# Nine normalizations of a three-block transformer pass taken in two token halves, with the GEMM blocks around each computed by halves

## The chip, the cores and the metric

The kernel runs on one core of a Trainium2 chip. Its engines are TensorE (PE in the profile, with PEld for its weight loads), VectorE (DVE), ScalarE (ACT), GpSimd (POOL) and SyncE (SP), which issues most DMAs. The metric is the device time of one execution in microseconds, as the median of several runs. Lower is better.

## The reference, cut to what matters

Two latent blocks and one further block are applied to 256 latent tokens, and in the first block to 256 context tokens as well, so 512 tokens ("both") up to the first half of the second block and 256 after it. The width is 1024. All in float32.

```python
x = x + 0.5 * mod[2] * swiglu(modulate(x, gain0, mod[0], mod[1]), ffn_a_in, ffn_a_out)
x = x + mod[5] * mixer(modulate(x, gain1, mod[3], mod[4]))      # attention + hyena, then retention
x = x + 0.5 * mod[8] * swiglu(modulate(x, gain2, mod[6], mod[7]), ffn_b_in, ffn_b_out)
# third block: plain rms_norm in place of modulate, a mixer, a cross attention, two swiglus
def modulate(x, gain, shift, scale):
    return rms_norm(x, gain) * (1 + scale) + shift
def rms_norm(x, gain):                       # over the 1024 features of each token
    return x * rsqrt(mean(x * x, -1) + 1e-6) * gain
```

Every residual update `x = x + gate * (h @ w_out)` is followed by a norm over the features of the whole new x, and that norm's result is the input of the next GEMM.

## The kernel before, in words

**Tiling.** x lies in SBUF with features on the partitions: `X[:, c, token]`, with eight chunks c of 128 features. A GEMM (one entry of `GEMMS`) is cut into blocks of 256 output features; a block has two tiles t of 128 features. Float32 accuracy is had from fp16: each weight tile `W` is split into `WH` (ACT, line 989, times 64) and the remainder `WL` (DVE, line 1362), each input into `XH` and `XL`, and `three` (lines 619 to 626) issues WH·XH, WH·XL, WL·XH. A block over kc chunks is 2·kc·3 matmuls, each with T columns (512 or 256 tokens). Most GEMMs have kc = 8 and so 48 matmuls a block; the outputs of the swiglus have kc = 11 in two parts, so 66 a block and 8 blocks.

**Residual GEMMs** (kind "resid", ten of them) have four output units u of two chunks. The last two units end in the last two blocks. DVE adds each unit to X (`add`, line 1477), ACT squares the new chunks (`squares`, line 1065), and POOL adds the squares of chunks 1 to 6 to that of chunk 0 (`pool_sums`, line 1778).

**The norm.** After the last block, PE adds the squares over the partitions (`pe_sums`, lines 594 and 601: 1 and 8 calls), DVE takes the reciprocal (line 1501), ACT the root (line 1095), PE spreads the result over the partitions (`pe_spread`, line 610: 4 calls). Each call is float32 and shows as two matmul records. Then, for each chunk, DVE multiplies (line 1518, "h"), ACT writes `XH` (line 1105, or 989 where there is no shift), DVE writes `XL` (line 1524 or 1526, "low"). PE's first block of the next GEMM waits for `XL` chunk by chunk; the later blocks don't.

**Order around the norm.** Each engine runs a written order; waits are on counting semaphores. Weights have two slots: the block k of the next GEMM can be split by ACT only when PE has left the same slot, so block 0 of the next GEMM after the second last block (`begin(after, (0,))`), and block 1 after the last (`begin(after, (1,))`). SP loads the next weights as soon as a slot of `W` has been split. In three of the GEMMs PE also computes modulation columns (`pe_mod`, lines 584 and 585) after each block, whose weights ACT and DVE split last after a norm (`begin_mods`).

The nine residual GEMMs named in the change and what follows each: ffn_0a_out (even_u), even_out (ffn_0b_in), ffn_0b_out (ffn_1a_in), ffn_1a_out (ret_q) with 512 tokens; ret_out (ffn_1b_in), ffn_1b_out (ffn_2a_in), ffn_2a_out (mix_q), mix_out (cross_q), cross_out (ffn_2b_in) with 256. Of these even_out, mix_out and cross_out have four blocks, ret_out eight, all with kc = 8. ret_q takes only the 256 latent tokens of the 512.

Of the kernel before, what the change touches and what calls it, by code (L numbers as in the profile page):

```python
# [131 lines left out]
def program(nc, io, out):  # L132
    ctx = ExitStack()
    with ctx:
# [108 lines left out]
        early_used, early_added = sem("early_used"), sem("early_added")  # L243
        h_ready, xh_ready, xl_ready = sem("h_ready"), sem("xh_ready"), sem("xl_ready")
# [57 lines left out]
        GEMMS = []  # L302

        def gemm(name, kind, w, kc, blocks, T, cols, rhs, parts=1, tok=False, dest=None, scale=1.0, gate=None, ffn=None, need=(), need_2=None, norm=None):
            g = dict(name=name, kind=kind, w=w, kc=kc, blocks=blocks, T=T, cols=cols, rhs=rhs, parts=parts, tok=tok,
                     dest=dest, scale=scale, gate=gate, ffn=ffn, units=blocks // parts, need=list(need), need_2=need_2, norm=norm, mods=0, m0=0, packed=name == "ret_g")
# [4 lines left out]
            if kind == "resid":  # L311
                g["r"] = sum(x["kind"] == "resid" for x in GEMMS)
                g["then"] = (1, 2, 3, 4, 5, 6, 7, 9, 10, 11)[g["r"]]
# [70 lines left out]
        def drained(g):  # L384
            return g["u0"] + g["units"]

# [86 lines left out]
        for n, N in enumerate(g["then"] for g in GEMMS if g["kind"] == "resid"):  # L473
            NORMS[N]["added"] = n + 1
        H0 = [0]
        for N in NORMS:
            H0.append(H0[-1] + DC * (N["T"] // SEQ))
# [95 lines left out]
        def _(pe):  # L573
# [15 lines left out]
            def pe_sums(n, chunks):  # L589
# [5 lines left out]
                for c in chunks:  # L595
                    if c == 0 and len(chunks) == 2:
                        pe.wait_ge(added_up, (DC - 2) * N["added"])
                    else:
                        pe.wait_ge(sq_ready, DC * n + c + 1)
# [5 lines left out]
            def pe_spread(n):  # L605

                q = NORMS[n]["T"] // 4
                pe.wait_ge(root_ready, n + 1)
                for j in range(4):
                    ins = mm(PS[:, BANK_N + 1, q * j:q * j + q], spread[j], root[:, 0:q], start=True, stop=True, skip_group_check=True)  # L610
                ins.then_inc(rstd_ready, 1)
# [5 lines left out]
            def pe_gemm(g, between={}):  # L617
                kc, T = g["kc"], g["T"]

                def three(dst, t, k, kp, c):  # L620
# [5 lines left out]
                    return mm(dst, wl, xh, start=False, stop=(kp == g["parts"] - 1 and c == kc - 1), skip_group_check=True)  # L626

                def one(k, kp, pair, w, u, first=False, early=False):
# [15 lines left out]
                    elif first and g["norm"] is not None:  # L644
                        pe.wait_ge(lo_ready, 2 * w + 2)
                        for c in range(kc):

                            pe.wait_ge(xl_ready, H0[g["norm"]] + c * (NORMS[g["norm"]]["T"] // SEQ) + T // SEQ)
# [13 lines left out]
                def turn_of(i, mods, first=False):  # L662
                    for b in range(2 * g["parts"]):
                        pair, kp = b // g["parts"], b % g["parts"]
                        one(b % 2, kp, pair, g["w0"] + b + 2 * g["parts"] * i, g["u0"] + pair + 2 * i, first and b == 0)
                        if mods:
                            pe_mod(g["m0"] + b + 2 * i, b)

                for s, v in g["need"]:
                    pe.wait_ge(s, v)  # L670
                if g["kind"] == "resid":
# [14 lines left out]
                if g["norm"] is not None:  # L686
# [139 lines left out]
            pe_gemm(gi["ffn_0a_out"], {b: lambda b=b: filter_step(b) for b in range(5)} | {7: lambda: pe.wait_ge(filt_ready, 5)})  # L826
# [160 lines left out]
        def _(act):  # L987
# [28 lines left out]
            def act_gemm(g, after, between={}):  # L1016
                n, T, u0 = g["blocks"] // 2, g["T"], g["u0"]

                def silu(i, k):
                    act.wait_ge(block_used, g["w0"] + k + 1 + 2 * i)  # L1020
                    act.activation(ffn_s[:, k, 0:T], PS[:, 2 * k, 0:T], ACT.Silu, scale=1.0 / W_SCALE).then_inc(silu_done, 1)  # L1021
# [18 lines left out]
                for lo, hi, mods in ((1, g["mods"], True), (max(g["mods"], 1), n, False)):  # L1040
                    if lo < hi:
                        with act.Fori(lo, hi) as i:
                            for k in range(2):
                                if is_ffn:
                                    silu(i - 1, k)
                                split(g, i, k)
                                if is_ffn:
                                    hidden(i - 1, k)
                                if mods:
                                    mod_split(g["m0"], i, k)  # L1050
# [16 lines left out]
            def act_resid(g, after, between={}):  # L1067
                n, nb, done = g["then"], g["blocks"], 0
                for b in range(2, nb):
                    split(g, b // 2, b % 2)  # L1070
                    while g["done"][done] <= b - 2:
                        squares(n, (2 * done, 2 * done + 1))
                        done += 1
                    if b in between:
                        between[b]()
                act.activation(warm[:, 1:2], mats[:, 1, 0:1], ACT.Sqrt)
# [6 lines left out]
                act_norm(n, after)  # L1083

# [7 lines left out]
            def act_root(n):  # L1092
                T = NORMS[n]["T"]
                act.wait_ge(inv_ready, n + 1)
# [797 lines left out]
```

## Time and profile before

| | us |
|---|---|
| median of 3 runs | 2673.7 (2672.0 to 2674.18) |
| the profiled execution | 2676.42 |
| its span, first to last instruction | 2674.6 |
| PE busy | 2545.5 (95%) |
| DVE busy | 1356.5 (51%) |
| ACT busy | 1091.2 (41%) |
| POOL busy | 247.1 (9%) |
| DMA, mean | 143 GB/s |
| granted PE clock, mean | 0.973 of full |

The profiled execution lies 1.8 us outside its span. PE is busy nearly always; since matmuls are pipelined, a matmul's shown length is more than the distance to the next one, and the distance is what counts. The granted clock of PE has two levels, 1.2 and 2.4 GHz, shown as 0.5 and 1.0 of full, and a window shows their mean.

### The profile page before, as it was taken

How to read it: one execution, taken by the hardware profiler on the slowest of the kernel's cores; microseconds unless marked ns; L12 is line 12 of the kernel's file. 1: busy time of each engine (PE TensorE's matmuls, PEld its weight loads, DVE VectorE, ACT ScalarE, POOL GpSimd, SP SyncE). 2: the span in 40 equal slices, each digit the busy share in tenths (PEclk: the TensorE clock that was granted, in tenths of full speed). 3: DMA queues.
4: the chain of work that ended last, by engine and by line, in shares of the span. 5: the costliest groups of instructions: out<-in, count | busy, mean ns of one | idle time of the engine just before them, and what ended most of it. 6: DMA issues, size and time to landing. Idle time of an engine off the chain costs nothing.

```text
span 2674.6 us, 45475 instructions
## 1 busy us (share of the span) xinstructions
PE 2545.5 (95%) x17855; PEld 1669.4 (62%) x17855; DVE 1356.5 (51%) x1911; ACT 1091.2 (41%) x1610; POOL 247.1 (9%) x235
## 2 busy tenths in 40 slices
PE   3899999999999999999999899999999999989999
PEld 3444444455644444444444568778888888777887
DVE  4755443453465553265532444365555654555664
ACT  5544423243354442254423321355444543444553
POOL 1810001004010000100003001021000010010001
PEclk7899999999999999999999899999999999999999
DMA  7976642330056673456643243238675764333574
GB/s 222 232 195 186 171 126 64 93 104 0 1 144 187 187 194 108 122 157 185 176 146 100 72 121 95 64 109 238 200 209 166 212 172 143 110 103 106 174 214 128
DMA packets 732734, 383.76 MB, mean 143 GB/s; under 512 B 12059, under 2 KB 729216, under 8 KB 732488
## 3 DMA queue, kind: packets, MB, share of 16 engines
q1 hardware_dynamic: 728312, 369.27, 49.2%
q0 software_dynamic: 3728, 10.98, 1.7%
q8 instruction: 86, 1.41, 0.2%
q10 hardware_dynamic: 576, 1.83, 0.2%
q14 instruction: 32, 0.26, 0.0%
HBM read 380.96 MB, written 1.08 MB: 143 GB/s over the span
## 4 chain that ended last, share of the span: by engine, by line
PE 87%; DVE 6%; DMA 3%; ACT 2%; issue 1%; POOL 0%; SPq 0%; ACTq 0%; DVEq 0%; POOLq 0%
PE PS L624 23%; PE PS L625 23%; PE PS L626 23%; DMA arena<-in_w_mod 2%; PE PS L735 2%; PE PS L643 1%; PE PS L642 1%; PE PS L641 1%; PE PS L761 1%; DVE WL L1362 1%; DVE arena L1518 1%; PE PS L909 1%; PE PS L601 1%; ACT WH L989 1%; PE PS L584 1%; PE PS L738 1%
## 5 line engine op out<-in xcount | busy, mean ns | idle before, releaser
L624 PE MATMUL PS<-XH,WH 128*128 128x256 f16 (+1 forms) x2912 | 948.6, 326 | 35.6 <-DVE XL L1524 21.0
L625 PE MATMUL PS<-XL,WH 128*128 128x256 f16 (+1 forms) x2912 | 948.1, 326 | 0.0
L626 PE MATMUL PS<-XH,WL 128*128 128x256 f16 (+1 forms) x2912 | 947.3, 325 | 0.0
L1362 DVE SCALAR_TENSOR_TENSOR WL<-W,WH 128x1024 f16<-128x1024 f32 (+1 forms) x520 | 666.0, 1319 | 287.1 <-ACT WH L989 287.0
L989 ACT ACTIVATE WH<-W 128x1024 f16<-128x1024 f32 (+1 forms) x520 | 551.2, 1107 | 611.7 <-PE PS L626 505.9
L624 PEld LDWEIGHTS PS<-XH,WH 128*128 128x128 f16 x2912 | 288.0, 99 | 224.5 <-issue 35.5
L626 PEld LDWEIGHTS PS<-XH,WL 128*128 128x128 f16 x2912 | 288.5, 99 | 181.8 <-issue 4.3
L625 PEld LDWEIGHTS PS<-XL,WH 128*128 128x128 f16 x2912 | 288.1, 99 | 171.3 <-issue 3.6
L624 PE MATMUL PS<-arena,WH 128*128 128x256 f16 (+1 forms) x1184 | 379.5, 321 | 0.8 <-DVE WL L1362 0.8
L625 PE MATMUL PS<-arena,WH 128*128 128x256 f16 (+1 forms) x1184 | 379.5, 321 | 0.0
L626 PE MATMUL PS<-arena,WL 128*128 128x256 f16 (+1 forms) x1184 | 379.4, 320 | 0.0
L1021 ACT ACTIVATE arena<-PS 128x512 f32<-128x512 f32 (+1 forms) x132 | 64.5, 489 | 552.2 <-PE PS L626 552.2
L1408 DVE SCALAR_TENSOR_TENSOR arena<-PS,arena 128x512 f32<-128x512 f32 (+1 forms) x132 | 73.6, 558 | 402.5 <-ACT arena L1021 402.5
L989 ACT ACTIVATE arena<-arena 128x1024 f16<-128x1024 f32 (+4 forms) x300 | 216.1, 761 | 52.9 <-DMA arena<-in_w_mod 23.4
L1778 POOL TENSOR_TENSOR arena<-arena 128x256 f32<-128x256 f32 (+1 forms) x60 | 80.0, 1334 | 1334.5 <-ACT arena L1065 1330.6
L1368 DVE SCALAR_TENSOR_TENSOR arena<-arena 128x1024 f16<-128x1024 f32 x144 | 172.6, 1237 | 23.3 <-ACT arena L989 23.3
L624 PEld LDWEIGHTS PS<-arena,WH 128*128 128x128 f16 x1184 | 116.1, 98 | 72.5 <-issue 3.3
L626 PEld LDWEIGHTS PS<-arena,WL 128*128 128x128 f16 x1184 | 116.1, 98 | 70.0
L625 PEld LDWEIGHTS PS<-arena,WH 128*128 128x128 f16 x1184 | 116.1, 98 | 69.5 <-issue 0.6
L1423 DVE TENSOR_SCALAR arena<-PS 128x1024 f32<-128x1024 f32 (+2 forms) x44 | 43.2, 982 | 177.7 <-PE PS L626 111.4
L989 ACT ACTIVATE arena<-PS 128x256 f32<-128x256 f32 (+1 forms) x117 | 49.3, 435 | 155.3 <-PE PS L751 86.0
L1477 DVE SCALAR_TENSOR_TENSOR X<-PS,modT,X 128x256 f32<-128x256 f32 x80 | 34.1, 479 | 154.3 <-PE PS L626 154.3
(232 smaller groups left out, 2317.1 us busy)
## 6 DMA issues: line engine op xcount, KB each, us to landing
arena<-in_w_mod SPq DMA_DIRECT2D x144, 512.0 KB, 6.8
W<-in_ffn_a_in SPq DMA_DIRECT2D x88, 512.0 KB, 4.9
W<-in_ffn_b_in SPq DMA_DIRECT2D x88, 512.0 KB, 4.8
W<-in_w_ffn_gu SPq DMA_DIRECT2D x88, 512.0 KB, 4.2
W<-in_ret_in SPq DMA_DIRECT2D x48, 512.0 KB, 4.4
W<-in_ffn_a_out SPq DMA_DIRECT2D x32, 704.0 KB, 5.6
W<-in_ffn_b_out SPq DMA_DIRECT2D x32, 704.0 KB, 5.7
W<-in_w_ffn_down SPq DMA_DIRECT2D x32, 704.0 KB, 5.6
```

What stands on the lines that cost most here:

```text
L624: mm(dst, wh, xh, start=(kp == 0 and c == 0), stop=False, skip_group_check=True)
L625: mm(dst, wh, xl, start=False, stop=False, skip_group_check=True)
L626: return mm(dst, wl, xh, start=False, stop=(kp == g["parts"] - 1 and c == kc - 1), skip_group_check=True)
L735: ins = mm(s, q, k, start=(c == 0), stop=(c == len(U["q"]) - 1 and U["bias"] is None), skip_group_check=True)
L989: return act.activation(dst, src, ACT.Copy, scale=scale)
L1021: act.activation(ffn_s[:, k, 0:T], PS[:, 2 * k, 0:T], ACT.Silu, scale=1.0 / W_SCALE).then_inc(silu_done, 1)
L1362: stt(WL[:, k, t, 0:g["kc"], :], W32[:, k, t, 0:g["kc"], :], W_SCALE, WH[:, k, t, 0:g["kc"], :], ALU.mult, ALU.subtract).then_inc(lo_ready, 1)
L1368: stt(MWL[k][:, t], M32[k][:, t], W_SCALE, MWH[k][:, t], ALU.mult, ALU.subtract).then_inc(mod_lo, 1)
L1408: stt(ffn_g[:, k, 0:T], PS[:, 2 * k + 1, 0:T], 1.0 / W_SCALE, ffn_s[:, k, 0:T], ALU.mult, ALU.mult)\
L1423: ts(dst, src, g["scale"] / W_SCALE, None, ALU.mult).then_inc(units_drained, 1)
L1477: ins = stt(X[:, c, tok], PS[:, 2 * (u % 2) + t, tok], gate, X[:, c, tok], ALU.mult, ALU.add)
L1778: tt(N["sq"][:, 0, 0:N["T"]], N["sq"][:, 0, 0:N["T"]], N["sq"][:, c, 0:N["T"]], ALU.add).then_inc(added_up, 1)
```

## The change

For the nine named residual GEMMs the tokens are taken in two halves of T/2 (256 of 512, or 128 of 256): half 0 and half 1.

- PE, tail: the units 2 and 3 are computed with matmuls of T/2 columns. The last block of each is done for half 0 first (`half_used`), then for half 1. The sums of half 0 stand inside the second last block's half 1, their spread inside the last block's half 1.
- PE, head: where the next GEMM has as many tokens, its blocks 0 and 1 are computed for half 0 (block 0 chunk by chunk as `XL` comes), then for half 1. The sums of half 1 stand between block 0 and block 1 of half 0, their spread inside block 1 of half 0. Where it has fewer (ret_q), block 0 waits for half 0 only; the sums of half 1 stand behind block 0 and their spread behind block 1.
- DVE and ACT: adds, squares, root, h, XH and XL go by halves. The split of block 1's weights stands inside the chunks of half 0.
- POOL: nine additions a norm in place of six, the last six of half the width.
- A wait for the hyena filter in ffn_0a_out moves from after block 7 to after block 5.

The core of the diff, first PE:

```diff
+                def half_three(k, kp, pair, t, c, s):
+
+                    H = T // 2
+                    xh, xl = g["rhs"](kp, c, T, kc)
+                    xh, xl = xh[:, H * s:H * s + H], xl[:, H * s:H * s + H]
+                    wh, wl = WH[:, k, t, c, :], WL[:, k, t, c, :]
+                    dst = PS[:, 2 * pair + s, H * t:H * t + H]
+                    mm(dst, wh, xh, start=(kp == 0 and c == 0 and t == 0), stop=False, skip_group_check=True)
+                    mm(dst, wh, xl, start=False, stop=False, skip_group_check=True)
+                    return mm(dst, wl, xh, start=False, stop=(kp == g["parts"] - 1 and c == kc - 1), skip_group_check=True)
...
+                    kp = g["parts"] - 1
+                    half_block(nb - 2, 2, kp, 1, (1, kc // 2), lambda: pe_half_sums(n, 0)).then_inc(block_used, 1)
+                    half_block(nb - 1, 3, kp, 1, (0, kc // 2), lambda: pe_half_spread(n, 0)).then_inc(block_used, 1)
+
+                def split_head():
+                    n = g["norm"]
+                    for s in range(2):
+                        for b in range(2):
+                            if s == 0:
+                                pe.wait_ge(units_drained, g["u0"] + b - 1)
+                                pe.wait_ge(lo_ready, 2 * (g["w0"] + b) + 2)
+                            for c in range(kc):
+                                if b == 0:
+                                    pe.wait_ge(xl_ready, H0[n] + DC * s + c + 1)
+                                for t in range(2):
+                                    ins = half_three(b, 0, b, t, c, s)
+                                if (s, b, c) == (0, 1, kc // 2):
+                                    pe_half_spread(n, 1)
+                            if s == 1:
+                                ins.then_inc(block_used, 1)
+                                if g["mods"]:
+                                    pe_mod(g["m0"] + b, b)
+                            elif b == 0:
+                                pe_half_sums(n, 1)
...
+                        if first and NORMS[g["norm"]]["halved"]:
+                            (pe_half_sums if b == 0 else pe_half_spread)(g["norm"], 1)
 
                 for s, v in g["need"]:
                     pe.wait_ge(s, v)
+                if g["split_tail"]:
+                    split_tail()
+                    return
```

ACT and DVE (`half_h`, `half_low`, `half_add` do for one half what lines 1518, 1524/1526 and 1477 did):

```diff
+                squares(n, range(2 * done, 4))
+                half_squares(0, 2)
+                half_squares(0, 3)
+                half_root(0)
+                begin(after, (0,))
+                half_squares(1, 2)
+                half_apply(0, range(0, 4))
+                half_squares(1, 3)
+                begin(after, (1,))
+                half_apply(0, range(4, DC))
+                half_root(1)
+                act.activation(warm[:, 0:1], mats[:, 1, 0:1], ACT.Silu)
+                half_apply(1, range(DC))
+                begin_mods(after)
...
+                half_add(0, 2)
+                dve.wait_ge(half_used, 2 * g["r"] + 2)
+                half_add(0, 3)
+                half_inverse(0)
+                dve.wait_ge(block_used, g["w0"] + nb - 1)
+                half_add(1, 2)
+                split(after, 0, 0)
+                dve.wait_ge(rstd_ready, M0[n] + 1)
+                for c in range(DC + 1):
+                    if c < DC:
+                        half_h(0, c)
+                    if c >= 1:
+                        half_low(0, c - 1)
+                    if c == 3:
+                        dve.wait_ge(block_used, g["w0"] + nb)
+                        half_add(1, 3)
+                        split(after, 0, 1, (0,))
+                    if c == 5:
+                        split(after, 0, 1, (1,))
+                half_inverse(1)
+                dve.wait_ge(rstd_ready, M0[n] + 2)
+                for c in range(DC + 1):
+                    if c < DC:
+                        half_h(1, c)
+                    if c >= 1:
+                        half_low(1, c - 1)
+                begin_mods(after)
```

**DVE, before**, at the end of ffn_1b_out and the start of the norm that follows (256 tokens). `X<-PS` are the adds of unit 3, `WL<-W,WH` a weight tile of the next GEMM (blocks 0 and 1), `arena<-X,pcol,PS` is h and `XL<-arena,XH` is low.

```order
L1362 SCALAR_TENSOR_TENSOR WL<-W,WH 128x1024 [waits hi_ready] x2
L1477 SCALAR_TENSOR_TENSOR X<-PS,modT,X 128x256 [waits early_used]
L1477 SCALAR_TENSOR_TENSOR X<-PS,modT,X 128x256 [waits block_used]
L1501 RECIPROCAL inv<-PS 128x64 [waits ms_ready]
L1362 SCALAR_TENSOR_TENSOR WL<-W,WH 128x1024 [waits hi_ready]
L1518 SCALAR_TENSOR_TENSOR arena<-X,pcol,PS 128x256 [waits rstd_ready]
L1518 SCALAR_TENSOR_TENSOR arena<-X,pcol,PS 128x256
L1526 TENSOR_TENSOR XL<-arena,XH 128x256 [waits xh_ready]
L1518 SCALAR_TENSOR_TENSOR arena<-X,pcol,PS 128x256
L1526 TENSOR_TENSOR XL<-arena,XH 128x256 [waits xh_ready]
L1518 SCALAR_TENSOR_TENSOR arena<-X,pcol,PS 128x256
L1526 TENSOR_TENSOR XL<-arena,XH 128x256 [waits xh_ready]
```

Both adds, the reciprocal and one tile of block 1 come before the first h; the second tile comes after four chunks.

**DVE, after**, at the same place, from h of chunk 3 of half 0 to the second tile of block 1. The columns are 128 in place of 256.

```order
L1725 SCALAR_TENSOR_TENSOR arena<-X,pcol,PS 128x128
L1734 TENSOR_TENSOR XL<-arena,XH 128x128 [waits xh_ready]
L1715 SCALAR_TENSOR_TENSOR X<-PS,modT,X 128x128 [waits block_used]
L1715 SCALAR_TENSOR_TENSOR X<-PS,modT,X 128x128
L1536 SCALAR_TENSOR_TENSOR WL<-W,WH 128x1024 [waits hi_ready]
L1725 SCALAR_TENSOR_TENSOR arena<-X,pcol,PS 128x128
L1734 TENSOR_TENSOR XL<-arena,XH 128x128 [waits xh_ready]
L1725 SCALAR_TENSOR_TENSOR arena<-X,pcol,PS 128x128
L1734 TENSOR_TENSOR XL<-arena,XH 128x128 [waits xh_ready]
L1536 SCALAR_TENSOR_TENSOR WL<-W,WH 128x1024 [waits hi_ready]
```

The adds of half 1's unit 3 and the first tile of block 1 now stand between chunk 3's h and chunk 3's low of half 0, behind a wait for the last block (`block_used`).

**ACT, before and after**, at the same place: `arena<-X` are squares, `WH<-W` weight tiles, `XH<-arena` the chunks of the norm. Before:

```order
L1065 ACTIVATE arena<-X 128x256 [waits units_drained] x2
L1065 ACTIVATE arena<-X 128x256 [waits early_added]
L1065 ACTIVATE arena<-X 128x256 [waits units_drained]
L989 ACTIVATE WH<-W 128x1024 [waits loaded_10,block_used]
L989 ACTIVATE WH<-W 128x1024 [waits loaded_11]
L1095 ACTIVATE root<-inv 128x64 [waits inv_ready]
L1089 ACT_TABLE_LOAD
L1089 ACTIVATE warm<-mats 128x1
L989 ACTIVATE XH<-arena 128x256 [waits h_ready] x8
```

After:

```order
L1226 ACTIVATE arena<-X 128x128 [waits half_added] x4
L1230 ACTIVATE root<-inv 128x32 [waits inv_ready]
L1106 ACTIVATE WH<-W 128x1024 [waits loaded_00,block_used]
L1106 ACTIVATE WH<-W 128x1024 [waits loaded_01]
L1226 ACTIVATE arena<-X 128x128 [waits half_added]
L1226 ACTIVATE arena<-X 128x128 [waits units_drained]
L1106 ACTIVATE XH<-arena 128x128 [waits h_ready] x4
L1226 ACTIVATE arena<-X 128x128 [waits half_added]
L1226 ACTIVATE arena<-X 128x128 [waits units_drained]
L1106 ACTIVATE WH<-W 128x1024 [waits loaded_10,block_used]
L1106 ACTIVATE WH<-W 128x1024 [waits loaded_11]
L1106 ACTIVATE XH<-arena 128x128 [waits h_ready] x4
```

Between XH of chunk 3 and of chunk 4 now stand two squares of half 1 and both tiles of block 1.

## Rows read from the trace of the kernel before

**Rows 1.** The page: chain that ended last, shares of the span by engine
```profile
PE 87%; DVE 6%; DMA 3%; ACT 2%; issue 1%; POOL 0%; SPq 0%; ACTq 0%; DVEq 0%; POOLq 0%
```

**Rows 2.** Waits of PE: who released it, us in total, times, longest
```profile
PE PS L624 <- DVE XL L1524: 21.0, 9, 6.7
...
PE PS L610 <- ACT root L1095: 12.6, 11, 1.4
PE PS L624 <- DVE XL L1526: 6.3, 4, 1.6
```

**Rows 3.** Windows of the nine transitions: length; busy (x) PE PEld DVE ACT POOL; clock; DMA
```profile
456.30:477.60 21.30, 16.65 (x76) 8.23 (x76) 16.74 (x37) 12.23 (x22) 0.00 (x0) 0.84 0.17 50
...
1506.00:1527.20 21.20, 14.46 (x76) 9.44 (x75) 16.74 (x37) 12.22 (x22) 0.00 (x0) 0.69 0.17 49
1828.60:1842.30 13.70, 10.59 (x77) 8.21 (x76) 9.82 (x20) 8.01 (x14) 3.74 (x4) 0.88 0.95 236
2010.60:2024.70 14.10, 11.59 (x77) 9.30 (x76) 9.34 (x20) 7.26 (x14) 0.00 (x0) 0.76 0.29 82
2192.30:2206.00 13.70, 11.19 (x77) 9.13 (x76) 9.28 (x20) 7.26 (x14) 0.00 (x0) 0.75 0.28 81
2406.40:2420.80 14.40, 11.43 (x77) 9.08 (x76) 9.28 (x20) 7.36 (x14) 0.72 (x1) 0.76 0.45 127
...
sum 155.10, PE 119.86 PEld 78.53 DVE 117.10 ACT 91.27 POOL 5.19; mean PE 13.32 PEld 8.73 DVE 13.01 ACT 10.14 POOL 0.58
```

**Rows 4.** Windows of PE alone inside a GEMM, 512 and 256 tokens
```profile
1090.00:1110.00 20.00, 20.00 (x94) 1.00 0.19 54
2040.00:2060.00 20.00, 20.00 (x185) 1.00 0.69 200
```

**Rows 5.** Timeline of PE, 512 tokens: start, length, line, shapes, count [idle before]
```profile
1138.59 1.16 PE L601 MATMUL PS<-arena,mats 128*128 128x128 f32 x8 [0.52 <-ACT arena L1065]
...
1144.93 0.38 PE L624 MATMUL PS<-XH,WH 128*128 128x512 f16 x1 [2.63 <-DVE XL L1524]
```

**Rows 6.** Timeline of PE, 256 tokens
```profile
2010.73 2.12 PE L601 MATMUL PS<-arena,mats 128*128 128x64 f32 x16
```

**Rows 7.** Timeline of PE in the modulation matmuls, 4 and 2 columns
```profile
90.43 0.17 PE L584 MATMUL PS<-silu_s,arena 128*128 128x4 f16 x1
90.46 0.16 PE L585 MATMUL PS<-silu_s,arena 128*128 128x2 f16 x1
```

**Rows 8.** Timeline of DVE, 256 tokens, then one row at 512
```profile
2016.24 0.48 DVE L1518 SCALAR_TENSOR_TENSOR arena<-X,pcol,PS 128x256 f32<-128x256 f32 x1
2016.63 0.42 DVE L1526 TENSOR_TENSOR XL<-arena,XH 128x256 f16<-128x256 f32 x1
2016.97 0.47 DVE L1518 SCALAR_TENSOR_TENSOR arena<-X,pcol,PS 128x256 f32<-128x256 f32 x1
...
2025.25 0.43 DVE L1408 SCALAR_TENSOR_TENSOR arena<-PS,arena 128x256 f32<-128x256 f32 x1 [2.85 <-ACT arena L1021]
2026.19 2.36 DVE L1362 SCALAR_TENSOR_TENSOR WL<-W,WH 128x1024 f16<-128x1024 f32 x2 [0.52 <-ACT WH L989]
...
788.68 0.68 DVE L1408 SCALAR_TENSOR_TENSOR arena<-PS,arena 128x512 f32<-128x512 f32 x1
```

**Rows 9.** Timeline of ACT, 256 tokens, then a pair of squares at 512
```profile
2003.56 2.00 ACT L989 ACTIVATE WH<-W 128x1024 f16<-128x1024 f32 x2 [3.04 <-PE PS L626]
2005.47 0.71 ACT L1065 ACTIVATE arena<-X 128x256 f32<-128x256 f32 x2
...
735.47 1.13 ACT L1065 ACTIVATE arena<-X 128x512 f32<-128x512 f32 x2
```

**Rows 10.** Windows of PE in the first block of ret_q, then its waits there
```profile
1517.30:1520.70 3.40, 1.60 (x12) 1.00 0.00 0
1520.70:1524.10 3.40, 2.48 (x11) 0.50 0.54 154
...
PE PS L624 <- DVE XL L1524: 4.4, 3, 1.9
```

More of the change, by code:

```diff
@@ L302, in program @@
         GEMMS = []
+        SPLIT_TAIL = ("ffn_0a_out", "even_out", "ffn_0b_out", "ffn_1a_out", "ret_out", "ffn_1b_out", "ffn_2a_out", "mix_out", "cross_out")
         def gemm(name, kind, w, kc, blocks, T, cols, rhs, parts=1, tok=False, dest=None, scale=1.0, gate=None, ffn=None, need=(), need_2=None, norm=None):
             g = dict(name=name, kind=kind, w=w, kc=kc, blocks=blocks, T=T, cols=cols, rhs=rhs, parts=parts, tok=tok,
[L306 removed]
+                     dest=dest, scale=scale, gate=gate, ffn=ffn, split_tail=name in SPLIT_TAIL, split_head=False, units=blocks // parts, need=list(need), need_2=need_2, norm=norm, mods=0, m0=0, packed=name == "ret_g")
             last = GEMMS[-1] if GEMMS else None
@@ L385, in drained, with halves @@
             return g["u0"] + g["units"]
+        for g, after in zip(GEMMS, GEMMS[1:]):
+            if g["split_tail"]:
+                after["split_head"] = after["T"] == g["T"]
+        def halves(T):
+            return [(s, s if T == BOTH else 0, slice(s * T // 2, (s + 1) * T // 2)) for s in range(2)]
         def segs(T):
@@ L685, in pe_gemm @@
                 n, mods, begin = g["units"] // 2, g["mods"], 0
-                if g["norm"] is not None:
+                if g["split_head"]:
+                    split_head()
+                    begin = 1
+                elif g["norm"] is not None:
                     turn_of(0, mods > 0, True)
@@ L1075, in act_resid @@
                         between[b]()
+                if g["split_tail"]:
+                    act_split_tail(g, after, done)
+                    return
                 act.activation(warm[:, 1:2], mats[:, 1, 0:1], ACT.Sqrt)
@@ L1458, in dve_gemm @@
                 else:
-                    if n > 1:
-                        with dve.Fori(1, n) as i:
+                    if g["split_head"]:
+                        for k in range(2):
+                            store(0, k, True)
+                            split(g, 1, k)
+                    if n > at:
+                        with dve.Fori(at, n) as i:
                             for k in range(2):
@@ L1480, in dve_resid @@
                 u = 0
+                if g["split_tail"]:
+                    for b in range(2, nb):
+                        while u < 2 and g["done"][u] <= b - 2:
+                            dve.wait_ge(block_used, g["w0"] + g["done"][u] + 1)
+                            add(u).then_inc(units_drained, 1)
+                            u += 1
+                        split(g, b // 2, b % 2)
+                        if b in between:
+                            between[b]()
+                    for u in range(u, 2):
+                        dve.wait_ge(block_used, g["w0"] + g["done"][u] + 1)
+                        add(u).then_inc(units_drained, 1)
+                    dve_split_tail(g, after)
+                    return
                 for b in range(2, nb + 1):
```

225 lines of the change are left out of this document (185 added, 40 removed).

## The prediction

> **What bounds the kernel now.** First the chain of waits: 87% of it is PE [rows 1], so a change pays by what it takes off PE's own row of work or out of PE's idle time. Then PE's waits: the norms stand first with 21.0 + 6.3 us before the next GEMM's first matmul and 12.6 us for the root [rows 2]. Then one window for each of the nine transitions, from the end of the last matmul of the residual GEMM to the start of the 49th of the next [rows 3]. Inside a GEMM a matmul starts every 20/93 = 0.215 us at 512 columns and every 20/183.5 = 0.109 us at 256 (a count in [rows 4] has one or two more, which overlap the edges). So 48 matmuls are 10.3 or 5.2 us. The nine windows last 155.1 us; three hold 48 matmuls of 512 and six of 256, 62.4 us. The loss is **92.7 us**: 11.0 at each of the three 512-token transitions (21.3 - 10.3), 16.0 at ret_q, and 8.5 to 9.2 at the five of 256 tokens, 44 together. The granted clock is 0.69 to 0.88 of full in those shown, so low-clock time is part of this loss.
>
> **Prices.** A float32 record of the norm: 8 take 1.16 us at 128 columns, and with the last one's own length of about 0.38 off that is 0.11 each [rows 5]; at 64 columns 16 take 2.12 [rows 6], so the price doesn't fall with the columns. I take 0.112 also for the 32 of the quarter size, bounded below by half of it. A 256-column matmul costs 0.109 and a 512 one 0.215, so a matmul has some 2.5 ns that columns don't explain, and one of 128 columns should take 0.056. No row has a float16 one of 128; below it is bounded by 0.053, above by the 256-column one's 0.109. I take 0.056 because matmuls of 4 and 2 columns, each with its own weights, start 0.03 apart [rows 7]: loading weights leaves room. By "TensorE: Matmul & The Clock Gate" of the Trainium skill (Wait — 56ns, not 53.3ns?), the sequencer spends about 62 ns on a matmul when decoding is not done in hardware, which would bind at 128 columns; some 2800 such matmuls at 6 ns more would be +17 us. Starts 0.03 us apart in [rows 7] say that this bound isn't there. On DVE h and low of 256 tokens start 0.39 and 0.34 apart, a weight tile takes 1.18, and 512 against 256 columns is 0.68 against 0.43 [rows 8]; so half the columns save 0.12 and leave 0.27 and 0.22. On ACT a weight tile is 1.0, a square 0.35 of 256 and 0.56 of 512 tokens [rows 9]; 0.25 for 128.
>
> **PE's own additions.** (a) A norm has 13 calls = 26 records, now twice: 52 × 0.112 = 5.8 us, all in PE's row of work. Before, 2.9 us of it were inside the loss. (b) More and shorter matmuls: 264 more in each of five swiglu outputs, 192 in ret_out, 96 in each of the other three, 96 in each of eight heads (not ret_q): 2568 × 2.5 ns = 6.4 us. Without any wait the nine transitions would lose 9 × 5.8 + 6.4 = 59 us, 34 less than now. The waits decide.
>
> **The walk at 256 tokens** (ffn_1b_out, clock at full). Time 0 is the end of the last block's half 0. The second last block's half 1 takes 66 × 0.056 = 3.7 plus the sums, 18 records, 2.0: done at 5.7. The last takes 3.7 plus the spread 0.9: done at 10.3. DVE: adds to 6.3; ACT splits block 0 at 5.8 to 7.8; DVE's two tiles 6.9 to 9.3; then h and low of chunks 0 to 2 to 11.0, the first low at 10.1, in time. Only then come the adds of half 1 (11.5), ACT's two squares (12.0), its first tile of block 1 (13.0), DVE's (14.3), h of chunk 4 and low of chunk 3 (14.8). PE is through with chunks 0 to 2 at 11.7 and sits idle for **3.2 us**. The second tile of block 1 before h of chunk 6 costs 1.2 more, and the chunks come 0.49 apart against 0.34 of PE. Block 0's half 0 ends at 18.2 in place of 13.0: 5.2 us of waiting. The sums of half 1 (to 20.2) and block 1 with the spread (to 23.8) cover root and reciprocal. Block 0's half 1 starts with the spread behind it and is paced by DVE: 1.3 us. The two halves of block 1 end at 30.5. The plain work in this stretch is 7.2 + 10.5 = 17.7, so 12.8 us are lost, and 0.5 for the extra matmuls before it: 13.3 against 8.9 now. What gates is work that had its place in the bubble before: two tiles of block 1 on both ACT and DVE, which can't start before PE leaves the slot.
>
> **The other transitions** by the same steps. ffn_2a: 13.3 against 8.5. The four-block ones of 256 tokens have half blocks of 48 matmuls, 1.0 us shorter each, so chunk 0 isn't ready when PE is: 1.5 more, 14.8 against 9.2 and 8.9. ret_out the same, with a shift in the norm (low 0.27 and not 0.22): 15.5 against 8.5. 512 tokens, ffn_0a: half blocks take 7.2, PE reaches block 0 at 17.3; chunks 0 to 2 last to 19.3; low of chunk 3 comes at 21.7 (two adds 0.8, square 0.4, tile 1.0, tile 1.2, h and low 0.8), later 1.3 for the second tile: 4.3 of waiting, 0.8 in half 1, 5.8 and 0.9 of PE's additions: 11.8 against 11.0. even_out and ffn_0b_out are followed by modulation tiles, split after half 1's last chunk, with PE there already: 1.5 more each, and 0.3 for the shorter block: 13.6 and 13.3 against 11.0. ret_q: the same 4.3 and 5.8 and 0.7, but the spread of half 1 stands behind block 1, and behind it DVE has 16 pieces (6.3), the drain of block 0 and the tile of block 2 (ACT 1.0, DVE 1.2): PE stands still for **9 us** before block 2. 19.8 against 16.0.
>
> Differences: 0.8 + 2.6 + 2.3 + 3.8 + 7.0 + 4.4 + 4.8 + 5.6 + 5.9 = **+37 us** at full clock.
>
> **The clock.** At 256 tokens each transition now has some 20 us in which PE is fed thinly: waits, sums of 32 columns, chunks paced by DVE. The nearest row is ret_q's first block, fed chunk by chunk: mean clock 0.69, and there it fell to 0.5 after a stretch of 3.4 us at full clock whose single waits were no longer than 1.9 us [rows 3, 10]. At 0.69 for 20 us, 12 us are at half; the stretch holds about 11 us of work, of which 0.6 is then doubled, +6.8, and the waits hide some 2.8 of it: +4 each, 20 us. At 512 tokens only the stretch after the first wait is thin: 3.4 us at half, +1.5 each, 6 us. Sum +26. Bounds: nothing, and 5 × 6.8 + 4 × 3 = 46.
>
> **Edits at nothing.** POOL's nine additions lie under PE's half block (only chunk 6 comes after half 0, about 0.7 us, against 2.0 or more until the sums). The filter's wait after block 5 comes 14 us after the fill of its last step; if that cover went it would cost one copy chain, under 4 us once. Loads of the next weights hang on the same splits and have the wait as slack.
>
> **Sum.** 2676.4 for the profiled execution + 37 + 26 = 2739; the median of the runs is 2.7 below the profiled one, so **2737 us**.
>
> **Rivals.** (A) Faster: the waits in the head don't come, because ACT and DVE have block 1's tiles done under half 0, and the clock never falls. Then 34 us less: 2640. For it speaks PE's reserve of 10.3 us in the two halves 0 at 512 tokens against some 7 us of DVE work; against it, the order: low of chunk 3 stands behind the tile, so reserve in block 1 is of no use to block 0. It decides only if the tile is ready within 2 us of the slot's release; squares, tile and tile alone are 2.6. 0.05. (B) The clock stays at full: +37, 2711. For it: no new wait but ret_q's is as long as the 6 to 8 us bubbles after which it fell. Against it: [rows 10]. The page above says (Why this matters for your kernels) that it is idle gaps of several microseconds between bursts that cost the clock; by that rule it would hold at eight of nine. 0.27. (C) My half-size prices are too high, the float32 records at 32 columns take half (5 × 52 × 0.056 = 15 us) and the clock stays: +22, 2696. 0.07. (D) A 128-column matmul is bound by its weight load and takes 0.09: 2800 × 0.034 = 95 us more, 2832. Against: [rows 7]. 0.03. (E) The change doesn't do what it says, the halves buy no earlier start and cost only PE's additions, about half of +37: 2692; the walk shows the first half in time at 512 tokens, 0.03. The forecast has 0.55, with its own range of 2722 to 2757.
>
> **The range** takes the forecast and B: 2700 to 2760. About 0.2% (5 us) is what a measurement of this kernel tells from no change. Faster 0.05 (A), same 0.03 (the near edges of C and E), slower 0.92.
>
> **What would show it.** In the changed profile: a wait of PE for the XL line of 2.5 to 3.3 us before chunk 3 at eight heads, one of about 1.3 before chunk 5, 9 us before ret_q's block 2; no wait for the root above 1 us; 0.112 us a float32 record and 0.056 a matmul of 128 columns; mean clock near 0.7 over the 256-token transitions. I am wrong if chunk 3 comes without a wait, if the clock stays at full, or if the 128-column matmul isn't at 0.056.

## The result: 64 us slower, and the profile after

| | before | after |
|---|---|---|
| median of 4 runs each, us | 2673.94 (2672.0 to 2675.97) | 2737.94 (2736.69 to 2740.07) |
| ratio to before | 1 | 1.0239, 95% interval 1.0223 to 1.0255 |
| span of the profiled execution, us | 2674.6 | 2736.7 |
| mean granted clock of PE | 0.973 | 0.966 |

The forecast was 2737, range 2700 to 2760. The page of the changed kernel: span, busy time by engine, and the shares of the chain that ended last.

```profile
span 2736.7 us, 51172 instructions
...
PE 2595.9 (95%) x20657; PEld 1851.2 (68%) x20657; DVE 1368.2 (50%) x2026; ACT 1106.9 (40%) x1695; POOL 253.7 (9%) x262
...
PE 88%; DVE 7%; DMA 2%; ACT 2%; issue 1%; SPq 0%; ACTq 0%; DVEq 0%
```

PE was 95% busy and is again; its share of the chain is 88% where it was 87% [rows 1]. It has 50 us more of shown busy time in a span 62 us longer. PE's waits in all (who released it, us in total, times, longest):

```profile
PE PS L676 <- DVE XL L1734: 16.9, 10, 3.0
PE PS L676 <- DVE XL L1732: 14.6, 9, 3.1
...
PE PS L665 <- DVE WL L1536: 11.6, 7, 8.8
...
PE PS L627 <- ACT root L1269: 2.3, 2, 1.4
```

Against [rows 2]: the waits for the root are all but gone (12.6 us to 2.3, the two norms outside the change). Two `XL` lines, L1734 without shift and L1732 with, have 16.9 and 14.6 us in pieces of at most 3.0 and 3.1, and L1536, the split of weights, has 11.6 with one of 8.8. They stand where the tail's bubble was, and are longer together: of the 21.0 us of [rows 2], 6.9 belong to the norm at the program's start, so before the nine transitions had some 20 us for `XL` and 10 for the root.

To see where the time went, one window for each transition, now from the first matmul of the last two units to block 2 of the next GEMM, which is a place that both kernels have. Columns: length; PE busy (matmul records); granted clock; DMA share; GB/s. Before (one of nine, ffn_1b_out's, and the sum):

```profile
1981.70:2029.90 48.20, 45.69 (x389) 0.93 0.50 140
...
sum 521.30, PE 485.37; mean PE 53.93
```

After, all nine in the order of the program:

```profile
392.20:490.30 98.10, 95.19 (x793) 0.98 0.24 67
744.60:801.20 56.60, 51.99 (x502) 0.97 0.46 126
1082.90:1177.70 94.80, 89.97 (x837) 0.96 0.35 101
1456.00:1543.20 87.20, 75.73 (x678) 0.95 0.23 66
1820.40:1871.40 51.00, 45.49 (x631) 0.87 0.70 201
2005.00:2061.90 56.90, 52.55 (x775) 0.91 0.39 112
2195.50:2252.90 57.40, 53.76 (x774) 0.85 0.40 112
2437.50:2477.70 40.20, 35.55 (x439) 0.79 0.34 98
2521.20:2560.20 39.00, 34.25 (x438) 0.82 0.35 100
sum 581.20, PE 534.48; mean PE 59.39
```

581.2 - 521.3 = **59.9 us** of the 62.1 by which the spans differ lie in these nine windows. Both kernels do the same useful work in a window (in ffn_0a's the hyena filter's too), so its growth is the extra loss of that transition:

| | tokens | window before, after | forecast, full clock + clock term | measured |
|---|---|---|---|---|
| ffn_0a | 512 | 97.1, 98.1 | 0.8 + 1.5 | 1.0 |
| even_out | 512 | 54.4, 56.6 | 2.6 + 1.5 | 2.2 |
| ffn_0b | 512 | 90.7, 94.8 | 2.3 + 1.5 | 4.1 |
| ffn_1a (ret_q) | 512 | 83.6, 87.2 | 3.8 + 1.5 | 3.6 |
| ret_out | 256 | 39.8, 51.0 | 7.0 + 4 | 11.2 |
| ffn_1b | 256 | 48.2, 56.9 | 4.4 + 4 | 8.7 |
| ffn_2a | 256 | 47.7, 57.4 | 4.8 + 4 | 9.7 |
| mix_out | 256 | 30.0, 40.2 | 5.6 + 4 | 10.2 |
| cross_out | 256 | 29.8, 39.0 | 5.9 + 4 | 9.2 |
| sum | | 521.3, 581.2 | 37 + 26 | 59.9 |

The place and the cause can be read at ffn_1b_out. PE (start, length, [idle before, released by]):

```profile
2041.99 0.23 PE L676 MATMUL PS<-XH,WH 128*128 128x128 f16 x1 [3.02 <-DVE XL L1734]
...
2046.34 3.60 PE L641 MATMUL PS<-arena,mats 128*128 128x32 f32 x16
```

DVE in the same stretch:

```profile
2034.06 2.36 DVE L1536 SCALAR_TENSOR_TENSOR WL<-W,WH 128x1024 f16<-128x1024 f32 x2 [0.48 <-ACT WH L1106]
2036.34 0.60 DVE L1725 SCALAR_TENSOR_TENSOR arena<-X,pcol,PS 128x128 f32<-128x128 f32 x2
...
2038.12 0.28 DVE L1734 TENSOR_TENSOR XL<-arena,XH 128x128 f16<-128x128 f32 x1
2038.32 0.60 DVE L1715 SCALAR_TENSOR_TENSOR X<-PS,modT,X 128x128 f32<-128x128 f32 x2
2040.25 1.23 DVE L1536 SCALAR_TENSOR_TENSOR WL<-W,WH 128x1024 f16<-128x1024 f32 x1 [1.32 <-ACT WH L1106]
2041.39 0.34 DVE L1725 SCALAR_TENSOR_TENSOR arena<-X,pcol,PS 128x128 f32<-128x128 f32 x1
2041.65 0.28 DVE L1734 TENSOR_TENSOR XL<-arena,XH 128x128 f16<-128x128 f32 x1
...
2042.32 1.22 DVE L1536 SCALAR_TENSOR_TENSOR WL<-W,WH 128x1024 f16<-128x1024 f32 x1
```

and ACT:

```profile
2038.70 0.57 ACT L1226 ACTIVATE arena<-X 128x128 f32<-128x128 f32 x2 [0.16 <-DVE X L1715]
2039.18 1.99 ACT L1106 ACTIVATE WH<-W 128x1024 f16<-128x1024 f32 x2
```

DVE's two tiles of block 0 end at 2036.4, then it runs through the first chunks; low of chunk 2 starts at 2038.12. The next low, of chunk 3, starts at 2041.65, with the two adds, 1.32 us of idle time for ACT, the tile L1536 and an h between them. ACT's two squares and its tiles from 2039.18 are the idle time. PE has done chunks 0 to 2 and sits idle for 3.02 us until 2041.99. The walk had 3.2. Behind the second tile (2042.32) comes the wait of 1.1.

### The profile page after: what moved, and what is told of

Read it like the earlier page. It is cut to its first block, busy times and chain, and to the rows that moved or that the text cites. A ratio compares the mean times of both kernels' runs of the same rounds, so it can differ in the third digit from the quotient of the medians.

```text
span 2736.7 us, 51172 instructions
## 1 busy us (share of the span) xinstructions
PE 2595.9 (95%) x20657; PEld 1851.2 (68%) x20657; DVE 1368.2 (50%) x2026; ACT 1106.9 (40%) x1695; POOL 253.7 (9%) x262
## 4 chain that ended last, share of the span: by engine, by line
PE 88%; DVE 7%; DMA 2%; ACT 2%; issue 1%; SPq 0%; ACTq 0%; DVEq 0%
PE PS L665 18%; PE PS L667 18%; PE PS L666 18%; PE PS L676 5%; PE PS L678 5%; PE PS L677 5%; DVE WL L1536 2%; DMA arena<-in_w_mod 2%; PE PS L852 2%; PE PS L641 1%; PE PS L749 1%; PE PS L747 1%; PE PS L748 1%; PE PS L878 1%; ACT WH L1106 1%; PE PS L1026 1%
## 5 line engine op out<-in xcount | busy, mean ns | idle before, releaser
L665 PE MATMUL PS<-XH,WH 128*128 128x256 f16 (+1 forms) x2560 | 831.7, 325 | 24.4 <-DVE WL L1536 9.8
L666 PE MATMUL PS<-XL,WH 128*128 128x256 f16 (+1 forms) x2560 | 831.2, 325 | 0.0
L667 PE MATMUL PS<-XH,WL 128*128 128x256 f16 (+1 forms) x2560 | 831.2, 325 | 0.0
L1536 DVE SCALAR_TENSOR_TENSOR WL<-W,WH 128x1024 f16<-128x1024 f32 (+1 forms) x520 | 661.3, 1310 | 297.6 <-ACT WH L1106 297.4
L667 PEld LDWEIGHTS PS<-XH,WL 128*128 128x128 f16 x2560 | 251.7, 98 | 160.9 <-issue 2.1
L676 PE MATMUL PS<-arena,WH 128*128 128x256 f16 (+1 forms) x1008 | 224.8, 247 | 0.0
L677 PE MATMUL PS<-arena,WH 128*128 128x256 f16 (+1 forms) x1008 | 224.8, 247 | 0.0
L678 PE MATMUL PS<-arena,WL 128*128 128x256 f16 (+1 forms) x1008 | 224.8, 247 | 0.0
L665 PE MATMUL PS<-arena,WH 128*128 128x256 f16 (+1 forms) x680 | 213.5, 314 | 1.9 <-DVE WL L1536 1.9
L667 PE MATMUL PS<-arena,WL 128*128 128x256 f16 (+1 forms) x680 | 213.4, 314 | 0.0
L666 PE MATMUL PS<-arena,WH 128*128 128x256 f16 (+1 forms) x680 | 213.4, 314 | 0.0
L676 PE MATMUL PS<-XH,WH 128*128 128x128 f16 (+1 forms) x704 | 167.4, 258 | 32.4 <-DVE XL L1734 16.9
L2049 POOL TENSOR_TENSOR arena<-arena 128x256 f32<-128x256 f32 (+2 forms) x81 | 79.3, 979 | 1230.7 <-ACT arena L1192 1002.6
L678 PE MATMUL PS<-XH,WL 128*128 128x128 f16 (+1 forms) x704 | 167.2, 258 | 0.0
L677 PE MATMUL PS<-XL,WH 128*128 128x128 f16 (+1 forms) x704 | 167.1, 258 | 0.0
```

The costliest lines, as they stand in the source:

```text
L665: mm(dst, wh, xh, start=(kp == 0 and c == 0), stop=False, skip_group_check=True)
L666: mm(dst, wh, xl, start=False, stop=False, skip_group_check=True)
L676: mm(dst, wh, xh, start=(kp == 0 and c == 0 and t == 0), stop=False, skip_group_check=True)
L677: mm(dst, wh, xl, start=False, stop=False, skip_group_check=True)
L1536: stt(WL[:, k, t, 0:g["kc"], :], W32[:, k, t, 0:g["kc"], :], W_SCALE, WH[:, k, t, 0:g["kc"], :], ALU.mult, ALU.subtract).then_inc(lo_ready, 1)
L2049: tt(N["sq"][:, 0, tok], N["sq"][:, 0, tok], N["sq"][:, c, tok], ALU.add).then_inc(added_up, 1)
```

## The experiments

Each was run beside the kernel before, and its difference is read from the ratio. The edits are abridged where three dots stand. The windows of an experiment come from one profiled execution each.

**e1: the halved matmuls alone.** On the kernel before; in the last two units and the next GEMM's first two blocks (eight heads):

```diff
-                    mm(dst, wh, xh, ...); mm(dst, wh, xl, ...); mm(dst, wl, xh, ...)
+                    for s in range(2):
+                        at = slice(s * T // 2, (s + 1) * T // 2)
+                        mm(dst[:, at], wh, xh[:, at], ...); mm(dst[:, at], wh, xl[:, at], ...); mm(dst[:, at], wl, xh[:, at], ...)
```

> The kernel before, with only one thing of the change: in the last two units of the nine residual GEMMs and in the first two blocks of the eight next GEMMs each matmul is issued as two of half the columns; norms, adds and order are as before. 2568 matmuls more. Fixed price per matmul of 2.5 ns: +6.4 us, so 2680 us. Rival, a matmul of 128 columns is bound by its weight load at 0.09 us: some 2800 of them at 0.034 more, about +90 us (2765). Second rival, the bubble after the tail hides nothing of it and the clock is unaffected in both cases.

Measured: 2676.49, ratio 1.0015 (1.0005 to 1.0024), so +4.0 us (1.3 to 6.4). The 6.4 of the sum stand at the upper end; 90 us are excluded. The changed kernel's own rate at 128 columns, in the tail of ffn_1b_out:

```profile
2008.00:2018.00 10.00, 10.00 (x183) 1.00 0.64 176
```

183 records, four of which began before the window (each is shown 0.22 us long), so 179 starts in 10 us: 0.056 each, as priced.

**e9: the second set of float32 records alone.** On the kernel before, after the first block of each residual GEMM:

```diff
+                        if b == 0 and g["name"] != "ffn_2b_out":
+                            for j in range(13):
+                                mm(PS[:, 5, 0:32], spread[j % 4], eps_mat[:, 0:32], start=True, stop=True, ...)
```

> The kernel before with 13 float32 calls of 32 columns (26 records) more after the first block of each of the nine residual GEMMs, into a bank nobody reads: the price of a second set of sums and spread in PE's row of work, alone. At 0.112 a record 2.9 us each, 26 in all: 2700. Rival, the price falls with the columns (0.056 or less): 13 or less, 2686.

Measured: 2700.77, ratio 1.0109 (1.0088 to 1.0130): +29 us (23.5 to 34.7). The group of the new records (line, shapes, count, busy us, mean ns):

```profile
L676 PE MATMUL PS<-mats 128*128 128x32 f32 x234 | 26.9, 273 | 0.0
```

234 = 9 × 26, and 29 / 234 = 0.12 us each (0.10 to 0.15); the 26 us of the forecast lie in the interval. The price does not fall with the columns: at 32 it is what it was at 128 [rows 5]. The rival with half the price is excluded by the interval.

**e2 and e11: the change at 512 tokens only, and at 256 only.** One edit, the list of GEMMs:

```diff
-        SPLIT_TAIL = ("ffn_0a_out", "even_out", "ffn_0b_out", "ffn_1a_out", "ret_out", "ffn_1b_out", ...)
+        SPLIT_TAIL = ("ffn_0a_out", "even_out", "ffn_0b_out", "ffn_1a_out")        # e2
+        SPLIT_TAIL = ("ret_out", "ffn_1b_out", "ffn_2a_out", "mix_out", "cross_out")  # e11
```

> The change at the four transitions of 512 tokens only; the five of 256 are as before. Theory of waits and clock, priced by transition: the 256-token ones cost some 48 us of the 63, so this is +11 to +15 us: 2687. Rival, the cost is the same at each transition because it is the second set of sums and the extra matmuls (7 us each): 4 x 7 = 28, so 2702.

> The complement of the 512-only run: the change at the five 256-token transitions only. If the costs add, the whole +64 less +11 leaves +49 to +53: 2722 to 2727. Rival, part of the cost belongs to both together (code, clock, loads): under 2715.

Measured: e2 2685.51, ratio 1.0042 (1.0027 to 1.0056), +11 us (7 to 15). e11 2721.25, ratio 1.0183 (1.0166 to 1.0201), +49 us (44 to 54). Together 60, against 64 (60 to 68): the costs add within their intervals. Equal cost at each transition (28 at 512 tokens) is out: four fifths are at the five of 256 tokens.

**e3: the split of block 1 moved behind half 0's chunks**, and with it half 1's last adds and squares. On the changed kernel, DVE (ACT likewise: all eight XH of half 0, then the squares and tiles):

```diff
                 for c in range(DC + 1):
                     ...
-                    if c == 3:
-                        dve.wait_ge(block_used, g["w0"] + nb)
-                        half_add(1, 3)
-                        split(after, 0, 1, (0,))
-                    if c == 5:
-                        split(after, 0, 1, (1,))
+                dve.wait_ge(block_used, g["w0"] + nb)
+                half_add(1, 3)
+                split(after, 0, 1)
```

> The changed kernel at all nine, with the adds of half 1, its squares and both weight tiles of block 1 moved behind all eight chunks of half 0 on ACT and DVE. Theory of waits: the wait before chunk 3 (about 3 us) and before chunk 5 (1.3) go at every transition; at 512 tokens nothing takes their place since block 1's tiles are ready before PE has done block 0's half 0 and the sums; at 256 tokens a wait of 1 to 2 us before block 1 comes instead. 4 x 4.3 + 5 x 3.5 = 34 us less than the change, and with the clock up for longer up to 20 more: 2690 to 2704. Rival, PE's own added work (second sums and spread, more matmuls) is the cost: within 5 us of the changed kernel's 2738.

Measured: 2699.67, ratio 1.0098 (1.0080 to 1.0116), so 38 us less than the change (some 31 to 44). The waits at ffn_1b_out's transition, all of them, where the changed kernel had 4.1 us in two for `XL`:

```profile
PE PS L676 <- DVE WL L1535: 1.2, 1, 1.2
PE PS L641 <- POOL arena L2045: 0.4, 1, 0.4
```

and windows of ffn_0a_out, ffn_0b_out and ffn_1b_out in this kernel, same ends as above:

```profile
388.90:482.60 93.70, 93.60 (x794) 1.00 0.25 71
1074.00:1162.50 88.50, 86.97 (x838) 1.00 0.38 109
1984.50:2036.50 52.00, 50.13 (x775) 0.97 0.43 123
```

The two windows of 512 tokens are 4.4 and 6.3 us shorter than in the changed kernel (98.1 and 94.8), and shorter than before too (97.1 and 90.7); at 256 tokens 52.0 against 56.9, and 48.2 before. By the same windows the other two of 512 tokens are 1.0 longer (even_out) and 0.8 shorter (ret_q) than before, and the other four of 256 tokens 2.7 to 6.2 longer. The wait before chunk 3 is gone and 1.2 us for block 1's tile comes in its place, as expected; at even_out, with its short half blocks, 1.0 us for that tile and 0.6 for POOL's sums come too, where nothing was expected. So the place of these adds, squares and tiles is worth 38 us of the 64, through the waits and through the clock (0.91 to 0.97 in the last row). Which of the three is worth what was not separated.

**e4: PE's waits filled at 256 tokens.** On the changed kernel, in block 0's half 0:

```diff
+                                if T == SEQ and (s, b) == (0, 0):
+                                    for _ in range({3: 12, 5: 4}.get(c, 0)):
+                                        mm(PS[:, 7, :], WH[:, 0, 0, 0, :], <WH[:, 0, 0, 0:4, :] as 512 columns>, start=True, stop=True, ...)
                                 if b == 0:
                                     pe.wait_ge(xl_ready, H0[n] + DC * s + c + 1)
```

> The changed kernel, with 12 matmuls of 512 columns before chunk 3 and 4 before chunk 5 of half 0 of the first block at four of the five 256-token transitions and the fifth alike (weights of the block as both operands, into a bank that nobody reads); they fill PE's waits and compute nothing that is used. Clock theory: low clock is 4 us or more of each 256-token transition's extra cost; with PE busy in the waits the clock stays at full longer, so 5 x 3 to 4 = 15 to 20 us less than the change: 2720. Rival, the clock costs nothing beyond the waits: the fill is at best hidden, 2738 to 2742.

Measured: 2710.56, ratio 1.0143 (1.0128 to 1.0158): 26 us less than the change (some 20 to 32), more than the 15 to 20 expected, by adding 80 matmuls that compute nothing. This separates the clock from the waits, since the fill computes nothing that is used and nothing comes earlier for it. In the five 256-token windows the changed kernel has some 72 us at half clock, worked out from the clock column above; the filled kernel's granted clock is full in all five transitions. Twenty microseconds around the wait before chunk 3 at ffn_1b_out's transition, first the changed kernel, whose row begins 0.8 us before the wait, then the filled one, whose row begins with the fill:

```profile
2038.00:2058.00 20.00, 15.79 (x153) 0.74 0.31 89
```

```profile
2027.90:2047.90 20.00, 19.23 (x231) 1.00 0.26 76
```

Clock 0.74 against 1.00, and 153 records against 231, of which 16 are the fill. In the changed kernel the stretch by pieces of 3.4 us:

```profile
2034.00:2037.40 3.40, 3.40 (x56) 1.00 0.16 46
2037.40:2040.80 3.40, 1.43 (x20) 1.00 0.90 263
2040.80:2044.20 3.40, 1.12 (x14) 0.89 0.39 113
2044.20:2047.60 3.40, 3.40 (x26) 0.50 0.68 198
2047.60:2051.00 3.40, 3.40 (x23) 0.50 0.00 1
2051.00:2054.40 3.40, 3.40 (x33) 0.60 0.00 0
2054.40:2057.80 3.40, 3.29 (x49) 1.00 0.02 5
```

Full through the wait of 3.02 us and the two chunks behind it; the fall comes in the second wait, and half clock lasts for the rest of block 0, the sums of half 1 and most of block 1, some 10 us in all: here low clock falls on work, not on waiting. The sums of 16 records took 3.60 us (the row at 2046.34) in place of 2.12 [rows 6].

**e7: ret_q's spread inside block 1.** On the changed kernel; `step` is called after chunk 4 of block 1's first tile:

```diff
-                            (pe_half_sums if b == 0 else pe_half_spread)(g["norm"], 1)
+                            pe_half_sums(g["norm"], 1)     # only behind block 0 (b == 0); the spread is now block 1's step
```

> The changed kernel with one line moved: at ret_q the spread of half 1 stands inside block 1 (after chunk 4 of its first tile) in place of behind it. The wait before ret_q's block 2 was 8.8 us and starts with that spread; 33 of block 1's 48 matmuls (3.6 us) now come after it: wait about 5.2, and the whole 3.6 us less than the change: 2734. Rival, the wait is one for the weights' load and not for DVE's sixteen pieces: no change.

Measured: 2733.45, ratio 1.0223 (1.0208 to 1.0238). The interval overlaps that of the change (1.0223 to 1.0255), so the time alone tells little; the wait does. First the changed kernel, then this one:

```profile
PE PS L665 <- DVE WL L1536: 8.8, 1, 8.8
```

```profile
PE PS L665 <- DVE WL L1539: 5.2, 1, 5.2
```

8.8 to 5.2: the 3.6 us forecast. Moving the spread alone shortened it by that much, so it runs from the spread through DVE's pieces and is not one for the weights' load. The two waits for `XL` in the same stretch grew from 2.6 to 3.4 us, so 2.8 of the 3.6 were left there.

**e8: the bubble of the kernel before, filled.** On the kernel before, 3 and 6 matmuls of 512 columns (5 and 10 at 512 tokens) before and behind the spread:

```diff
                     pe_sums(g["then"], (0, DC - 1))
+                    fill(g["then"], 3 if T == SEQ else 5)         # at the nine alone
                     pe_spread(g["then"])
+                    fill(g["then"], 6 if T == SEQ else 10)
```

> The kernel before with PE's waits in the nine bubbles partly filled by matmuls whose result nobody reads (3 and 6 of 512 columns at 256 tokens, 5 and 10 at 512, before the spread and before the next GEMM). Clock theory: low clock after the bubble is gone or shorter. At 512 tokens the first block is paced by DVE's chunks (1.6 us a chunk against 1.3 of PE), so nothing is won there; at 256 tokens up to 1 us each: 4 to 6 us less, 2668. Rival, the low clock after the bubble costs half its length everywhere (9 x 1.7 to 3.4 = 20 us): 2653. Third, the fill costs as much as it gives: 2673.

Measured: 2668.50, ratio 0.9989 (0.9980 to 0.9998): 2.9 us less (0.5 to 5.3). PE in the bubble behind ffn_1b_out:

```profile
2006.73 0.81 PE L609 MATMUL PS<-mats 128*128 128x512 f16 x3
2007.83 1.10 PE L616 MATMUL PS<-root,mats 128*128 128x64 f32 x8 [0.29 <-ACT root L1106]
2008.77 1.46 PE L609 MATMUL PS<-mats 128*128 128x512 f16 x6
2010.51 0.27 PE L630 MATMUL PS<-XH,WH 128*128 128x256 f16 x1 [0.28 <-DVE XL L1537]
```

The last row is the next GEMM's first matmul, at the full-clock length of 0.27. All the low clock is gone at eight of the nine. From the first record of the sums to the 90th matmul of the next GEMM, the filled kernel takes as long as before, to 0.01 us, at ffn_0a_out, even_out, ffn_0b_out and ret_out, 1.7 us less at ret_q and 0.9 to 1.4 less at the other four of 256 tokens. These add up to 6.3 us in the one profiled execution, which took 2665.12 us where the median is 2668.50; the interval above is what the times show. The rival of 20 us is out: before, low clock fell mostly on a block that waited for DVE anyway.

**e6 and e10: versions that beat both.** e6 is e2 with e3's and e7's edits: halves at 512 tokens only, late split, ret_q's spread inside block 1. e10 adds e8's fill at the 256-token transitions.

> The change at the four 512-token transitions only, with the late split (adds and squares of half 1 and block 1's tiles behind half 0's eight chunks) and, at ret_q, the spread of half 1 inside block 1 in place of behind it; the five transitions of 256 tokens as before. From the ledger of the late-split run: -3.5 at ffn_0a, +1.0 at even_out, -2.2 at ffn_0b, -0.8 at ffn_1a, and some 4 more there for the earlier spread: -9 to -10 us, so about 2664, faster than both kernels. Rival, the gains at 512 tokens are of the size of the noise of such a ledger: within 3 us of 2673.

> The faster version of the 512-token transitions (late split, ret_q's spread inside block 1), and in the five 256-token ones the order of before with PE's waits filled as in the filled kernel. If the two gains add: 5.1 and 3 to 4 us, 2664. Rival, the fill gained only by chance of noise, or at 512 tokens: 2667 as without it.

Measured: e6 2667.03, ratio 0.9981 (0.9972 to 0.9990), 5 us faster than before; e10 2667.45, ratio 0.9971 (0.9960 to 0.9982), 8 us faster. The intervals of the two overlap, so that the fill adds to it is likely and not shown. e6's four windows:

```profile
388.60:482.30 93.70, 93.61 (x793) 1.00 0.25 71
738.10:795.20 57.10, 53.99 (x502) 0.94 0.48 133
1076.90:1167.00 90.10, 88.56 (x836) 0.98 0.40 112
1445.30:1524.40 79.10, 73.89 (x677) 0.99 0.25 72
```

against 97.1, 54.4, 90.7 and 83.6 before: 3.4 and 4.5 less at ffn_0a and ret_q, 0.6 less at ffn_0b, but 2.7 more at even_out. The expectation was -9 and the time gave -5; e6 fell short at even_out and ffn_0b, the two whose next GEMM splits modulation tiles after the norm. Why their clock fell there in this execution (0.94) and less in e3's (0.97) was not pursued.

## Why the prediction was right

The time was hit within 1 us. That is luck beyond some 5 us: the parts at 512 tokens were priced 4.5 us too high, and at 256 tokens the clock too low and the rest too high. By its own steps:

- **What bounds, and the loss before.** Right: 59.9 of 62.1 us lie in the nine windows.
- **PE's additions.** The float32 records were priced at 26.2 us for nine second sets (9 × 2.9); e9 measured 29 alone (23.5 to 34.7). The working took 0.38 us off for the last record, which is the length of a float16 matmul of 512 columns; a float32 record is shown 0.28 long, but the records start 0.112 apart in the trace, so the price holds. The matmuls were priced at 6.4; e1 measured 4.0 (1.3 to 6.4). 128 columns cost 0.056, as priced.
- **The walk.** Its main wait was 3.2 us and is 3.02; the 9 us at ret_q are 8.8, and e7 showed from where they run. That the waits come from what stands inside half 0's chunks is shown by e3, which moved half 1's adds, squares and block 1's split together and took 38 us off.
- **512 tokens.** Forecast 9.5 at full clock and 6 for the clock, 15.5; e2 has 11 (7 to 15). The waits for `XL` behind ffn_0a_out were 2.4 and 0.5 us. The steps written down give 2.4 (21.7 - 19.3) before chunk 3 and 1.3 before chunk 5, which is 3.7; the sum has 4.3, so 0.6 of it at each of the four transitions has no working. The first wait was right and the second overpriced. What low clock costs at 512 tokens was not measured alone.
- **256 tokens.** Forecast 27.7 at full clock and 20 for the clock; e11 has 49 (44 to 54). Filling the waits alone gave 26 us back (20 to 32), so low clock cost about 26 and the rest about 23: the clock term was too small, though 20 is at the edge of that interval. The forecast was 12 us at half clock at each of the five transitions. The clock column gives some 10 at ffn_1b, 14 at ret_out and cross_out and 17 at ffn_2a and mix_out, 72 in all against 60. Of these 72, 36 would be lost if PE's own work had paced all of it, and 26 came back, so some 2 us each were hidden where the forecast hid 2.8.
- **Rivals.** A (the waits don't come) is out: they came, though e3 shows that at 512 tokens it needs only another order. B (the clock stays at full) is out by the piecewise row: it fell after a wait of 3.02 us and in one of 1.1. C (float32 records at half price) is out by e9, D (weight load binds at 128 columns) by e1. E (halves buy no earlier start) is out as a time. Its price doesn't follow from its condition either: PE's additions alone were priced at 32.6 us, which makes 2706 and not 2692. What it says is half true. The first chunk came almost in time at ffn_1b_out (0.3 us) and the waits for the root went. But in e3, with the late order, this transition still loses 3.8 us more than before, 12.7 against 8.9, and 3.8 is just what PE's additions come to there (2.9 for the records, 0.9 for 360 more matmuls at the forecast's 2.5 ns). So of the 6.0 us of waiting and low clock that the kernel before has there beside its records, nothing was won back. At ffn_0a_out the additions are the same 3.8 us and the window is 3.4 shorter, so 7.2 of some 8 were.

Why halves pay at 512 tokens and not at 256 is in part argued. DVE takes 512 tokens in pieces of 256 in both kernels, but 256 tokens in pieces of 128 after the change. With them a chunk takes it 0.46 us (2037.40 to 2037.86 above) where the whole chunk took 0.73 (2016.24 to 2016.97, [rows 8]), while PE's share of a chunk went from 0.65 to 0.33. So DVE's work for a norm grew, and it paces PE more; the two weight tiles, 1.2 us each, stay whole besides. No run separates these.

## What to carry to other kernels

Splitting a serial step in two to hide it doubles its fixed costs. Count on every engine the instructions whose price doesn't fall, or falls less than the work: here 26 records of 0.11 us on PE, and DVE's chunks at 0.46 us in place of half of 0.73. The bubble being larger than the added records is not enough: it was 8.9 us a time at 256 tokens, against 3.8 of additions, and no order that was tried made the split pay there; at 512 tokens it was 11 to 16, and the split paid at three of four once its order was right (e3). When work moves out of a bubble, look for what else lived in the bubble: here the split of the next block's weights, with half 1's adds and squares, which then stood ahead of the data that PE wanted. Moving that work for a later block behind the last piece of the earlier one gave 38 us here.

## What the runs showed of the hardware

- A float32 matmul record of the norm (each call is two) costs 0.11 to 0.12 us at 32, 64 and 128 columns alike.
- A float16 matmul of 128 columns starts every 0.056 us with a weight load for each; 2568 more matmuls, by halving ones of 512 or 256 columns, cost 4.0 us (1.3 to 6.4), 0.5 to 2.5 ns each.
- PE's clock fell to half at ffn_1b_out after waits of 3.02 and 1.1 us with 12 short matmuls between them, and stayed there for some 10 us while PE was busy. Eighty useless matmuls in the waits kept it at full and made the kernel 26 us faster.
- Half clock costs little where another engine paces PE: e8 took it away at three transitions of 512 tokens and at ret_out and won nothing there, and 2.9 us (0.5 to 5.3) in all.
